# Prompt attention of a hybrid decoder: rounds of three groups in place of two, and another placing of the scores between them

## The reference

```python
l_c = einsum('bqgrd,bcgd->bgrqc', q, kc) * scale + bias_c;  p_c = masked_softmax(l_c, d_c >= 0)
l_s = einsum('bqgrd,bgqkld->bgrqkl', q, k_sel) * scale + bias_s;  p_s = masked_softmax(l_s, m_s)
l_w = einsum('bqgrd,bwgd->bgrqw', q, kw) * scale + bias_w;  p_w = masked_softmax(l_w, m_w)
o = gates[..., 0:1] * (p_c @ vc) + gates[..., 1:2] * (p_s @ v_sel) + gates[..., 2:3] * (p_w @ vw)
```

## Time and profile before

| | |
|---|---|
| median of three runs | 3126.16 us |
| the profiled execution | 3130.0 us |
| its span, first to last instruction | 3128.2 us |
| mean granted clock | 0.966 of full speed |
| TensorE / VectorE / ScalarE / GpSimd busy | 2970.6 / 1567.1 / 816.7 / 954.9 us |
| prompt attention in the span | about 436 to 848 us |

### The profile page before, as it was taken

The page is one execution under the profiler, slowest core; times in us unless marked ns, Lnnn a source line. Parts: engine busy times, 40 slices in busy tenths (PEclk is TensorE's granted clock), DMA queues, the critical chain, the costliest instruction groups (busy, mean ns, idle before and its releaser), DMA issues. The chain is left out here.

```text
span 3128.2 us, 51259 instructions
## 1 busy us (share of the span) xinstructions
PE 2970.6 (95%) x19425; PEld 2755.5 (88%) x19425; DVE 1567.1 (50%) x3487; ACT 816.7 (26%) x1509; POOL 954.9 (31%) x420
## 2 busy tenths in 40 slices
PE   7999979999989889999999999999999999999998
PEld 7999956666666689999999999897899999999998
DVE  6211137777644424761653726396347616526362
ACT  5002016776733312330210202123223302102020
POOL 4330000000000034444444444451244444444443
PEclk9997979999989999999999999999999999999999
DMA  6116650000156421111111111312111111111112
GB/s 188 45 40 219 218 185 1 2 1 2 46 171 192 152 92 52 40 41 47 47 37 51 40 48 39 120 46 104 55 52 41 38 50 42 43 50 36 52 36 88
DMA packets 128367, 222.66 MB, mean 71 GB/s; under 512 B 15930, under 2 KB 91936, under 8 KB 127028
## 3 DMA queue, kind: packets, MB, share of 16 engines
q1 hardware_dynamic: 108232, 201.47, 20.0%
q10 hardware_dynamic: 19980, 19.14, 2.3%
HBM read 202.51 MB, written 22.18 MB: 72 GB/s over the span
## 5 line engine op out<-in xcount | busy, mean ns | idle before, releaser
L382 POOL TENSOR_SCALAR weights_high<-weights_whole 128x1024 fp32r<-128x1024 f32 (+2 forms) x168 | 436.0, 2595 | 1064.5 <-PE banks L417 889.5
L413 PE MATMUL banks<-ffn_in_high,weights_high 128*128 128x364 f32 (+1 forms) x2112 | 468.5, 330 | 17.0 <-DVE ffn_in_low L280 9.3
L415 PE MATMUL banks<-ffn_in_low,weights_high 128*128 128x364 f32 (+1 forms) x2112 | 467.8, 330 | 0.0
L417 PE MATMUL banks<-ffn_in_high,weights_low 128*128 128x364 f32 (+1 forms) x2112 | 466.1, 329 | 0.0
L413 PEld LDWEIGHTS banks<-ffn_in_high,weights_high 128*128 128x128 f32 x2112 | 367.4, 189 | 19.1 <-issue 19.1
L2751 DVE SCALAR_TENSOR_TENSOR conv_out<-conv_ext,conv_w,conv_out 128x1024 f32<-128x1024 f32 x176 | 321.4, 1826 | 111.1 <-ACT conv_out L2687 97.5
L384 POOL TENSOR_TENSOR weights_low<-weights_whole,weights_high 128x1024 fp32r<-128x1024 f32 (+2 forms) x168 | 366.5, 2181 | 24.7 <-issue 0.6
L417 PEld LDWEIGHTS banks<-ffn_in_high,weights_low 128*128 128x128 f32 x2112 | 368.2, 189 | 0.0
L415 PEld LDWEIGHTS banks<-ffn_in_low,weights_high 128*128 128x128 f32 x2112 | 367.9, 189 | 0.0
L2687 ACT ACTIVATE conv_out<-conv_ext,conv_b,conv_w 128x1024 f32<-128x1024 f32 (+1 forms) x176 | 138.6, 836 | 543.0 <-DVEq L2742 542.9
L2779 DVE TENSOR_TENSOR x<-x,banks 128x728 f32 (+1 forms) x128 | 86.5, 718 | 385.1 <-PE banks L417 385.1
(11 more groups left out here) (433 smaller groups left out, 4665.1 us busy)
## 6 DMA issues: line engine op xcount, KB each, us to landing
weights_whole<-in_w_up SPq DMA_DIRECT2D x88, 512.0 KB, 3.5
past_rows<-in_kv_pages SPq DMA_DIRECT2D x160, 128.0 KB, 2.3
z<-in_kv_pages SPq DMA_DIRECT2D x96, 128.0 KB, 2.4
weights_whole<-in_w_down SPq DMA_DIRECT2D x32, 384.0 KB, 3.1
weights_whole<-in_w_down SPq DMA_DIRECT2D x32, 320.0 KB, 2.9
x<-in_cmp_pages ACTq DMA_DIRECT2D x64, 128.0 KB, 5.8
x<-in_cmp_pages SPq DMA_DIRECT2D x64, 128.0 KB, 5.4
cmp_rows<-in_cmp_pages ACTq DMA_DIRECT2D x64, 128.0 KB, 5.4
```

The lines of the kernel that those rows point to most:

```text
L382: pool.tensor_scalar(high, whole, 1.0, None, ALU.mult)
L413: pe.matmul(o, wh, high[:, at], start=kk == 0, stop=False)
L415: pe.matmul(o, wh, low[:, at], start=False, stop=False)
L417: last = pe.matmul(o, wl, high[:, at], start=False, stop=kk == len(terms) - 1)
```

## The change

A constant `BATCH = 3` takes the place of the two groups of a round. A round now issues three groups' turns, three groups ahead, then three groups' values; `probs_turned` has six slots in place of four; the PSUM banks for turns are still three and those for scores still three. `starts` is 1 above a multiple of three. A score whose index is a multiple of three goes ahead of the round's turns, and every other one between turns and values. ScalarE places a unit's output five copies (`LAG`) after the unit's last group in place of three.

```diff
--- before.py
+++ after.py
@@ -1145,6 +1145,7 @@
     NEAR = 2 * P
     SMALL = 4 * P
     RING = 3
+    BATCH = 3
     PERIODS = [(i, x) for i in range(R) for x in range(QT // 2)]
     NP = len(PERIODS)
     PHASES = 6
@@ -1160,7 +1161,7 @@
         nmx = k.sb(ctx, "negated_maxima", [P, 2 * RING, G * 3])
         sums = k.sb(ctx, "sums", [P, 2 * RING, G * 3])
         coef = k.sb(ctx, "coefficients", [P, 2 * RING, G * 3])
-        pt = k.sb(ctx, "probs_turned", [P, 4, 512])
+        pt = k.sb(ctx, "probs_turned", [P, 2 * BATCH, 512])
         third = z[:, Z_KC:Z_GATE, :].rearrange("p a n -> p (a n)")
         third_sel = third[:, 0:G * SEQ].rearrange("p (g n) -> p g n", g=G)
         third_win = third[:, G * SEQ:G * (SEQ + WK)].rearrange("p (g n) -> p g n", g=G)
@@ -1212,10 +1213,10 @@
             groups += group_list(u)
             ends.append(len(groups))
         NGR = len(groups)
-        NB = -(-NGR // 2)
+        NB = -(-NGR // BATCH)
 
         places = {}
-        starts = [0] + [2 * ((ends[2 * p + 1] - 1) // 2) - 1 for p in range(NP)]
+        starts = [0] + [BATCH * ((ends[2 * p + 1] - 1) // BATCH - 1) + 1 for p in range(NP)]
         for p in range(NP - 2):
             for f in range(PHASES):
                 places.setdefault(starts[p] + f * (starts[p + 1] - starts[p]) // PHASES, []).append((p + 2, f))
@@ -1309,7 +1310,7 @@
                     for g in range(G):
                         d = group_rows(g)
                         w, v = {"s": (P, k.vals[:, 0, tile, d]), "w": (P, k.vals[:, 1, tile, d]), "c": (NCP, comp_v[0:NCP, B, d])}[what]
-                        last = pe.matmul(out(u)[d, :], v, pt[0:w, a % 4, (2 * y + g) * P:(2 * y + g + 1) * P],
+                        last = pe.matmul(out(u)[d, :], v, pt[0:w, a % (2 * BATCH), (2 * y + g) * P:(2 * y + g + 1) * P],
                                          start=first and y == 0, stop=what == "c")
                 if group[-1][0] == "c":
                     last.then_inc(valued, 1)
@@ -1319,15 +1320,16 @@
                     score(p, f)
             for j in range(-1, NB):
                 if j >= 0:
-                    for p, f in places.get(2 * j, ()):
+                    for p, f in places.get(BATCH * j, ()):
                         score(p, f)
-                turn(2 * j + 2)
-                turn(2 * j + 3)
+                for x in range(BATCH):
+                    turn(BATCH * (j + 1) + x)
                 if j >= 0:
-                    for p, f in places.get(2 * j + 1, ()):
-                        score(p, f)
-                    values(2 * j)
-                    values(2 * j + 1)
+                    for x in range(1, BATCH):
+                        for p, f in places.get(BATCH * j + x, ()):
+                            score(p, f)
+                    for x in range(BATCH):
+                        values(BATCH * j + x)
 
         @block.vector
         def _(dve):
@@ -1483,6 +1485,7 @@
                 return step
 
             STEPS = 5
+            LAG = 2 * BATCH - 1
 
             def copy(a):
 
@@ -1491,7 +1494,7 @@
                 full = sum(what != "c" for what, _, _ in group) * 2 * P
                 for rows, first, end in ((P, 0, full), (NCP, full, len(group) * 2 * P)):
                     if first < end:
-                        last = act.activation(pt[0:rows, a % 4, first:end], turned_bank(a)[0:rows, first:end], ACT.Copy)
+                        last = act.activation(pt[0:rows, a % (2 * BATCH), first:end], turned_bank(a)[0:rows, first:end], ACT.Copy)
                 last.then_inc(copied, 1)
 
             def place(u):
@@ -1511,13 +1514,13 @@
                 for r in range(count):
                     a = at + r
                     copy(a)
-                    if a - 3 in [e - 1 for e in ends]:
-                        place(ends.index(a - 2))
+                    if a - LAG in [e - 1 for e in ends]:
+                        place(ends.index(a - LAG + 1))
                     for x in range(total * r // count, total * (r + 1) // count):
                         ahead[x // STEPS](x % STEPS)
                 at += count
             for u in range(UN):
-                if ends[u] - 1 + 3 >= NGR:
+                if ends[u] - 1 + LAG >= NGR:
                     place(u)
```

## The result

The changed kernel took 3185.16 us (the median of five runs) against 3126.16. The medians differ by 59 us, but one of the five runs fell in a slower state of the chip (4204.72 us at a granted clock of 0.645), and without it the ratio to before is 1.0171, 95% interval 1.0155 to 1.0186: slower by about 53 us. The prediction had the sign, but 20 us for the size: 3146, and its range ended at 3176. The profiled execution has a span of 3183.3 us against 3128.2.

The account below looks back on a forecast made before the run. VectorE and TensorE hold each other through three score banks. First period 16, 14 x 15.95, 7 x 16.6 and 13.2 of late exponentials: 368.7 against 351.8 us, +17; ends +3: +20, so 3146 us, range 3108 to 3176.

Parts of the forecast that it names:

- Pairs without cover: Scores placed back to back: the second waits for VectorE's first take; TensorE's waits for takes up from 21.5 to 50 us or more.
- Late exponentials: In 8 of 14 periods of 9, ScalarE's exponentials reach VectorE's second weigh 1.5 us late; 13.2 us in all.
- periods of 12: Periods (six scores of one head pair's two query tiles) whose start advances 12 groups: 7 of 21, forecast 16.6 us each.
- The clock: TensorE's clock in the stretch of placed scores, read as 0.99 of the 2.4 GHz level and counted as no term.
- The deduction: 0.45 us taken off each worked period, then scaling by 16.0/16.45: 15.95 us at 9 groups, 16.6 at 12.
- periods of 9: Periods (six scores of one head pair's two query tiles) whose start advances 9 groups: 14 of 21, forecast 15.95 us each.
- Six slots and the later placing at nothing: Six slots for turned probabilities and outputs placed five copies later: both counted at 0 us, bounds -20 and 32.
- The seam: From a period's last score to the next one's first take: VectorE's idle up from 1.05 to 2.06 us.
- A: Rival: TensorE's own chain sets the pace, so 21 us of switches between kinds of work come off: 3105 us; 22%.
- B: Rival: switches and copies' waits saved equal the pair waits: 3126 us, towards 3103 with all copies' waits gone; 18%.
- C: Rival: placing outputs holds ScalarE, late exponentials grow to 3.0 us in every period of 9: 3175 us; 15%.

Follow-up runs that it names:

- e5: The changed kernel with the second score of each pair placed behind the values of the round's first group; 3161.38 us, ratio to before 1.0104.
- e1: The changed kernel with 16 extra transposes ahead of the wait of the period's last score (S5) in the 14 periods of 9; 3170.18 us, ratio 1.0137.
- e9: e5 with the extra transposes of e1 added; 3151.67 us, ratio to before 1.0080.
- e7: The kernel before with six slots of turned probabilities and not four; 3127.53 us, ratio to before 0.9994.
- e4: The changed kernel with a unit's output placed six copies after its last group and not five; 3184.59 us, ratio to before 1.0173.
- e6: e5 with the large tile's exponentials behind the period's first three copies and not the first five; 3137.0 us, ratio to before 1.0035.
- e3: The changed kernel with each period's start at a multiple of three, 2 groups later; 3119.35 us, ratio to before 0.9969.
- e10: e3 with the edit of e5; 3114.47 us, ratio to before 0.9948.

## Why the prediction was wrong, point by point

*Pairs without cover.* Right in mechanism and in the row: 1.88 forecast, 1.89 measured for S1; TensorE's waits 63.4 us for "50 or more". e5 shows that it costs some 21 us, of which up to 8 are clock (lost clock 27.4 to 18.8).

*Late exponentials.* Right in mechanism, and the eight periods were the right ones; two periods of 12 were late as well. VectorE's waits are 19.2 us for "towards 20". In the period shown the wait is 2.98 where 2.7 was the sum for two missing copies.

*The clock: the step that failed.* The prediction read 0.99 in the row of before and wrote "so it is no term here". But it forecast in the same text that TensorE would stand idle before S5 for 1.3 us and 1.5 more in eight periods, which before's trace shows nowhere (its longest such wait there is 1.6). A clock that the trace shows at the full level under short waits says nothing of a kernel with waits twice as long. The term was there in small in before's own trace: one period took 18.02 us where four others with the same work and the same waits took 16.45 or 16.46, 1.57 more for 1.6 of lost clock.

```profile
661.61:678.06 16.45, 14.84 (x140) 10.06 (x140) 12.45 (x71) 11.57 (x31) 0.00 (x0) 1.00 0.00 1
726.09:744.11 18.02, 16.41 (x140) 11.36 (x140) 12.44 (x71) 11.58 (x31) 0.00 (x0) 0.91 0.01 1
```

Lost clock went from 1.7 to 27.4 us. At the 0.9 to 1.0 us that these pairs give for each, that is an estimate of 23 to 26 of the 35 us which the forecast was short (20 for the 55 of the profiled spans). e1 and e9, which change only what TensorE does while it waits, give some 11 and 8 us back, net of the filler's own work. The Trainium skill (TensorE: Matmul & The Clock Gate, HAM oscillation) says that long idle gaps of TensorE, there waits for a DMA, lower its clock for what follows; the trace agrees, with 0.56 over the 7.8 us behind the 4.15 us wait, and shows the same behind waits shorter than the gaps that the page speaks of, 0.53 over the 7 us behind one of 2.10.

*The deduction.* The steps applied to before's order gave 16.9 us for a period that took 16.45, and 0.45 was taken off each period afterwards, then 2.8% more. In the period shown the steps without it give S5 at 15.87 where it came at 15.86. Where the clock held and no exponential was late, periods of 9 took 15.5 to 16.9 us, a mean of 16.2 against 15.95 (the raw steps had 16.8); the three periods of 12 at full clock took 16.2, 18.0 and 18.6, a mean of 17.6 against 16.6, where the raw steps had 17.5. So the deduction was wrong above all for the periods of 12: with 0.3 us in 14 periods and 1.0 in 7, some 11 us in all. That the remaining third of the error lies there is an estimate from few periods, not shown by a run. (One figure beside it is a slip: 888 is the count for both key groups, so it stands against 960 places, or 444 against 480; the sum doesn't use it.)

*Six slots and the later placing at nothing.* Both right as far as tested: e7 (in the kernel before), e4 (one copy later still, with ScalarE's wait for values gone).

*The seam.* Forecast 2.06 us of VectorE's idle for 1.05; 1.80 to 2.12 at full clock. e6, with pairs parted and exponentials in time, still stands 9 us above before; e3, which shortens the seam to values alone, lies 9 below. The seam is the one thing that e3 cures and e6 leaves, but e3 differs from e6 in the scores' other places as well, so the 18 us between them are not all shown to be its own.

*The rivals.* A (the switches set the pace) was wrong for this kernel: the time rose although 21 us of switches were saved. In e3 and e10, where TensorE waits less for takes than before (18.5 and 17.8 us), the change brings 9 and 14 us; that this is the switches' share is not shown. B fell with the sign. C's sign of being decisive (ScalarE's waits for values over 20 us) was not there, 14.8, and e4 shows those waits cost nothing.

## What to carry to other kernels

Two engines that hold each other through a few buffers are paced by what stands between the steps of the exchange: before rounds are made larger, write down what will lie between each pair of such steps, and place the exchange's steps anew, since an offset of two groups in one formula was worth 63 us here. Where a forecast makes TensorE's waits longer than any that the trace has, price the lower clock behind each as well; to find out what it costs, look for the same stretch of work at both levels of the clock in one trace, and fill the wait with idle work. A cure for a late step (exponentials earlier) is worth trying only in the kernel that has it: it gained some 21 us in one order and lost 17 in the other.

## What the runs showed of the hardware

Work added to a waiting TensorE made the kernel faster: 224 transposes into a free PSUM bank, some 11 us off. Of the changed kernel's ten waits of 2.1 to 4.2 us before S5, nine were followed by a lowered clock (0.52 to 0.76 over the next 7 us; in one such stretch 10 transposes took 2.40 us), and one of 2.59 us was not, while a second of 2.59 was. Of the waits up to 1.6 us most were not; one of 1.27 us, and one of 1.37 in the kernel before, were (0.76 both times). So the length of the last wait alone does not settle it. The lower clock cost 0.9 to 1.0 us for each microsecond lost.
